# Retention outputs of layer 1 from centred values, with copies and squares moved to VectorE

## The chip, the cores and the metric

The kernel runs on one core of a Trainium2 chip. The metric is device time in microseconds of one execution. Engines: PE is TensorE (matmuls), DVE is VectorE, ACT is ScalarE, POOL is GpSimd, SP is SyncE, which here issues loads.

## The reference

One inference step of a 2-layer decoder, for a prompt of 256 tokens and 8 sample tokens that share all weights (264 columns in all, model width 1024). Each layer has three branches side by side (an S5 state space, stick-breaking attention and retention), then an output projection with a residual and a layer norm, then a feed-forward part with a short convolution. The change is in the retention branch of layer 1, whose core is this:

```python
def retention_branch(q, k, v, g, pos, s0, gn_g, gn_b):
    ...
    s_new, o = lax.scan(step, s0.astype(F32), (to_chunks(q), to_chunks(k), to_chunks(v)))
    o = o.swapaxes(0, 1).reshape(bn, L, RET_HEADS, RET_DV)
    mu = jnp.mean(o, -1, keepdims=True)
    var = jnp.mean(jnp.square(o - mu), -1, keepdims=True)
    o = ((o - mu) * lax.rsqrt(var + LN_EPS)).reshape(bn, L, RET_WIDTH) * gn_g + gn_b
    return jax.nn.silu(g) * o, s_new
```

Within a prompt, the output of a head is a weighted sum of value rows (`inner` times `v`), so its mean over the head's 128 features is the same weighted sum of the rows' means. The samples' outputs come from the state and the new value row. The other two branches end in an RMS norm.

## The kernel before

Features lie on the partitions, tokens in the columns: every activation is a tile of 128 x 264 (256 prompt columns, then 8 of samples). The weights are cut into units of 128 x 1024 that SP loads into a ring of five. A layer has 20 input units (`N_IN`), 8 output units (`N_OUT`), 44 up and 22 down. From unit 16 of layer 1 on, a weight is split in a rounded high half (ACT, `split_hi`) and the rest (DVE, `split_lo`), and each block is three matmuls: high by high, high by low, low by high.

Every engine has its own program, written out by hand, with semaphores between them (`need`, `E.did`). The table `AT` says behind which input tile `i` of a layer a step stands, and each engine goes through its steps in the order of its text; within an engine nothing overtakes. PSUM has eight banks, and `claim` waits for the last reader of a bank.

The tail of layer 1's input phase goes like this. Behind tile 16, TensorE turns the samples' outputs (`ret_samples_turn`, `sb_values_turn`), then transposes the value rows (`transposes`) and the samples' values (`v_samples`). ACT copies the values from PSUM to `VT` (`v_tokens`), copies the samples' rows and sends them to DRAM (`v_spread`); POOL fetches them back, spread over partitions, as `VBC` (`v_rows_back`). Behind tile 17, TensorE makes the retention outputs of the four heads from `VT` and the decayed scores `RI` (`ret_out`); ACT copies them into `Oh`, opens the first two gates (`open_gates`, with a table load on either side) and squares the second branch (`square_b`). Behind tile 18, TensorE multiplies `Oh` with a matrix of 1/128 for the means (`gn_means`), DVE subtracts them (`gn_center`), ACT squares, TensorE means again for the variance (`gn_vars`); between these stand the two branches' sums of squares (`rms`, which wait for `square_sum` on DVE). ACT takes logarithm and exponential into `rg`. Then come tile 19, the prompt's retention state (`ret_state`), and the output projection, whose first three tiles are done in two halves over the branches: `cat_hi` and `cat_lo` are their high and low halves, made by `branch_hi` on ACT and `branch_lo` on DVE behind `gn_scale` and `gn_out`.

DVE also updates the samples' retention states in `SR`, two operations for each of eight samples (`ret_states`); they wait for `VBC`. `STATES[L]` says which samples are done where: (4, 8) in layer 1 puts samples 0 to 3 ahead of the centring, 4 to 7 ahead of the branches' scaling, and none behind the splits. When all are done, POOL stores `SR` (1 MB). Behind the last low half DVE makes the low half of output unit 23 and adds the residuals; TensorE waits for the first of these (`z`) before it shifts the next norm and goes on to the fourth output.

Of the kernel before, what the change touches and what calls it, by code (L numbers as in the profile page):

```python
# [63 lines left out]
UP_BANKS = 8  # L64
SHIFTED = [4, 3]
END_BANK = [7, 0, 1, 2]
STATES = [(3, 5), (4, 8)]
SILU = [3, 2]
AHEAD = {j: 6 if j <= 24 else 4 for j in range(6, N_UP + 4)}
CSLOTS = 8  # L70
S5_ACT = [4, 6, 8]
# [35 lines left out]
def hybrid_step(nc, A, O):  # L107
    with ExitStack() as ctx:
# [12 lines left out]
        def at(name, shape, over=None, dt=F32):  # L121
# [4 lines left out]
            else:  # L126
# [33 lines left out]
        xe_hi = at("xe_hi", [P, KT, T], over=("z", 0), dt=F32R)  # L160
        ring_lo = at("ring_lo", [P, RING, 8, P], over=("ring", 0), dt=F32R)
        we_hi = [at(f"we_hi{e}", [P, 8, P], over=(home, plane * HJ * T), dt=F32R)
                 for e, (home, plane) in enumerate((("work", 0), ("work", 1), ("turn", 0), ("turn", 1)))]
        tabs = [(turn[:, 0, :, 0:SEQ], turn[:, 1, :, 0:SEQ]), None]
        RI = at("RI", [P, HEADS, DEC])
        KD = at("KD", [P, 2, 256])
        VT = at("VT", [P, 2, HEADS * DV])
# [46 lines left out]
        rope = at("rope", [P, 2, T])  # L214
        steps = at("steps", [P, SEQ])
        kdec = at("kdec", [P, 2, HEADS])
        vrow = at("vrow", [P, DV])
        gam = at("gam", [P, 1])
        gcol = at("gcol", [P, RAW, 2])
# [187 lines left out]
        def _(pe):  # L407
# [260 lines left out]

            def ret_out(L):
                need(pe, "vt", L, 2)  # L670
                for h in range(HEADS):
                    need(pe, "ri", L, h + 1)
                    bank = claim(OUT_BANK[h], "oev", L, h + 1)
                    mm(bank[:, 0:SEQ], VT[:, 0, h * DV:(h + 1) * DV], RI[:, h, 0:SEQ], start=True, stop=False)
                    E.did(mm(bank[:, P:SEQ], VT[:, 1, h * DV:(h + 1) * DV], RI[:, h, SEQ:DEC], start=False, stop=True),
                          "ro")

            def gn_means(L):
                need(pe, "osamp", L, 1)
                for h in range(HEADS):  # L680
                    need(pe, "oev", L, h + 1)
                    bank = claim(4 + h, "gd", L, h + 1)
                    E.did(mm(bank[:, 0:T], C["mean_v"], Oh[:, h], start=True, stop=True), "gmean")

            def gn_vars(L):
                for h in range(HEADS):
                    need(pe, "gsq", L, h + 1)
                    bank = claim(4 + h, "gv1", L, 1)
                    E.did(mm(bank[:, 0:T], C["mean_v"], sqo[:, h], start=True, stop=True), "gvar")

# [100 lines left out]
            for L in range(DEPTH):  # L791
# [7 lines left out]
                for i in range(RAW, N_IN):  # L799
                    out = claim(in_bank(i), "in_evac", L, i - RAW + 1)[:, 0:T]  # L800
                    if i in EARLY[L]:
                        tile8_split(L, i, out)
                    else:
                        tile8(L, i, out, lambda k: x[:, k],
                              (lambda k: need(pe, "x", L, k + 1)) if i == RAW else None)
                    for hf in range(2):
                        for c in range(2):
                            if i == at_[f"b{hf}{c}"]:
                                s5_b(L, hf, c)
                    if i == at_["ss"]:  # L810
# [24 lines left out]
                    if i == at_["sv"]:  # L835
                        sb_sample_values(L)
                    if i == at_["values"]:
                        sb_values(L)
                    if i == at_["rsq"]:
                        ret_samples(L)  # L840
                    if L == 0 and i == at_["out"]:
                        ret_out(L)
                    if i == at_["rt"]:
                        ret_samples_turn(L)
                    if i == at_["yt"]:
                        sb_values_turn(L)
                    if L > 0 and i == at_["vt"]:
                        transposes(L)
                    if L > 0 and i == at_["vb"]:
                        v_samples(L)  # L850
                    if L > 0 and i == at_["out"]:
                        ret_out(L)
                    if i == at_["gmean"]:
                        gn_means(L)
                    if i == at_["rms"]:
                        rms(L, sqa, 1, "rmsl", "rms", 2)
                        rms(L, sq2, 2, "rmsl", "rms", 3)
                    if i == at_["gvar"]:
                        gn_vars(L)
# [81 lines left out]
        def _(act):  # L941
# [14 lines left out]
            def split_hi_early(L, i):  # L956

                n = L * UNITS + i
                act.wait_ge(S(f"ld_w{ring_slot(n)}"), 16 * (n // RING + 1))
                need(act, "s5rd", L, 2)  # L960
                E.did(nc.scalar.copy(we_hi[EARLY[L].index(i)][:], ring[:, ring_slot(n)]), "w_hi")

            def upper_early(L):
# [182 lines left out]
            def v_tokens(L):  # L1146

                for tt in range(2):
                    need(act, "trv", L, tt + 1)
                    E.did(nc.scalar.copy(VT[:, tt], ps[:, 4 + tt]), "vt")  # L1150

            def v_spread(L):
                need(act, "vb", L, 1)
# [45 lines left out]
            for L in range(DEPTH):  # L1199
                at_ = AT[L]  # L1200
                ln_in(L)
                for i in range(RAW, N_IN):
# [82 lines left out]
                    if i == at_["out"]:  # L1285
# [3 lines left out]
                        if L == 0:  # L1289
                            square_a(L)  # L1290
                            split_hi(L, N_IN + 2)
                    if L > 0 and i == 17:
                        open_gates(L)
                        square_b(L)
                    if i == at_["gmean"]:
                        if L == 0:
                            square_b(L)
                        for h in range(HEADS):
                            need(act, "gd", L, h + 1)
                            E.did(f(sqo[:, h], Oh[:, h], ACT.Square), "gsq")  # L1300
                        if L > 0:
                            split_hi(L, N_IN + 2)
# [5 lines left out]
                    if i == at_["gvar"]:  # L1308
                        need(act, "gvar", L, HEADS)
                        E.did(f(rg[:], ps[:, 4:8, 0:T], ACT.Ln, bias=eps_t[LN_EPS]), "gv1")  # L1310
                        E.settle()
                        E.did(f(rg[:], rg[:], ACT.Exp, scale=-0.5), "gr")
                        for k in range(4):
                            branch_hi(L, k)
                E.settle()
                gates = hb[:, GC + SILU[L]:GC + HEADS]
                E.did(f(gates, gates, ACT.Silu), "gsil")
# [65 lines left out]
        def _(dve):  # L1383
# [504 lines left out]
            def sb_cat(L):  # L1888
                need(dve, "rmsr", L, 1)
                for t in range(2):  # L1890
                    E.did(stt(hb[:, QB_ + t], yb[:, t], pv(L, "norm_b_g", t), rms2[:, 1], ALU.mult, ALU.mult), "catb")

            def gn_center(L, heads):
# [17 lines left out]
            def branch_lo(L, k):  # L1911

                need(dve, "cat_hi", L, k + 1)
                E.did(tt(cat_lo[:, k], cat[k], cat_hi[:, k].bitcast(F32), ALU.subtract), "cat_lo")  # L1914

            def s5_skip(L, hf):
# [32 lines left out]
            for L in range(DEPTH):  # L1949
# [45 lines left out]
                    ret_states(L, range(0, STATES[L][0]))  # L1995
                else:
                    split_lo(L, N_IN)
                sample_out(L)
                sb_sample_out(L)
                if L > 0:  # L2000
                    split_lo(L, N_IN + 1)
                square_sum(L, 0)
                if L > 0:
                    ret_states(L, range(0, STATES[L][0]))
                gn_center(L, (0, 1))
                square_sum(L, 1)
                gn_center(L, (2, 3))
                if L == 0:
                    split_lo(L, N_IN + 1)
                ret_states(L, range(STATES[L][0], STATES[L][1]))  # L2010
# [244 lines left out]
```

## Time and profile before

| | us |
|---|---|
| median of 3 runs | 677.65 (677.31 to 677.99) |
| the profiled execution | 677.52 |
| its span, first to last instruction | 675.7 |

| engine | busy us | share of the span |
|---|---|---|
| TensorE, matmuls | 664.1 | 98% |
| VectorE | 566.6 | 84% |
| ScalarE | 415.7 | 62% |
| GpSimd | 90.7 | 13% |

The span is what the profiler saw of that execution; the rest of its time lies before the first and behind the last instruction. Times below are microseconds from the span's start. TensorE's granted clock is full in the whole span. Busy shares are averages; where an engine stands is seen only in the views of waits and of the chain, and when it does what in the timeline. In a timeline, instructions of one kind that follow each other are merged, "x8" is their count, and the time beside it is from the first start to the last end, or the sum where they overlap; a float32 matmul shows as two records.

### The profile page before, as it was taken

Reading aid. Unit: us, or ns where it says so; the run is one execution under the profiler, and the core shown is the slowest. Engines: PE = TensorE matmul, PEld = TensorE weight load, DVE = VectorE, ACT = ScalarE, POOL = GpSimd, SP = SyncE. Lnnn points to the kernel's source line nnn. Section 1 sums busy time; section 2 is a strip of 40 time slices with the busy share of each in tenths; the row PEclk is TensorE's granted clock in tenths of the full one; section 3 lists DMA queues with packets and bytes.
Section 4 is the critical chain, followed back from the end, with each engine's and each line's share of the span. In section 5 each row is a group of like instructions: output and inputs, shape, how many; then the busy total and the mean of one; then the engine's idle time right before and its main releaser. Section 6 shows DMA issues by size and latency. Waiting matters only on the chain. (4 is left out here: it accounts for less than half of the span.)

```text
span 675.7 us, 13394 instructions
## 1 busy us (share of the span) xinstructions
PE 664.1 (98%) x5030; PEld 615.2 (91%) x5030; DVE 566.6 (84%) x1191; ACT 415.7 (62%) x682; POOL 90.7 (13%) x90
## 2 busy tenths in 40 slices
PE   9999999999999999999999999899999999999997
PEld 7777887989999999999977887889999999999996
DVE  6999999989998988789489998688999898884653
ACT  5776258767765766645756445687767666663343
POOL 0000010140222211200200000105012222220001
PEclk9999999999999999999999999999999999999999
DMA  8776630746574555554365662454765545555411
GB/s 326 247 258 219 200 117 5 287 109 234 200 258 150 206 188 184 180 186 152 125 207 198 191 207 100 129 215 137 192 207 205 188 161 200 177 193 191 159 59 65
DMA packets 42916, 121.82 MB, mean 180 GB/s; under 512 B 5539, under 2 KB 15171, under 8 KB 42339
## 3 DMA queue, kind: packets, MB, share of 16 engines
q1 hardware_dynamic: 40466, 115.22, 49.5%
q0 software_dynamic: 1088, 4.11, 2.6%
q10 hardware_dynamic: 1296, 1.63, 0.8%
q8 instruction: 40, 0.66, 0.4%
q14 instruction: 26, 0.21, 0.1%
HBM read 115.33 MB, written 5.61 MB: 179 GB/s over the span
## 5 line engine op out<-in xcount | busy, mean ns | idle before, releaser
L1556 DVE TENSOR_TENSOR w_lo<-ring,w_hi 128x1024 fp32r<-128x1024 f32 x144 | 175.6, 1221 | 31.6 <-ACT w_hi L954 29.8
L436 PE MATMUL ps<-x_hi,w_hi 128*128 128x264 f32 x672 | 191.0, 284 | 1.0 <-DVE x_lo L1506 1.0
L437 PE MATMUL ps<-x_lo,w_hi 128*128 128x264 f32 x672 | 190.4, 283 | 0.0
L438 PE MATMUL ps<-x_hi,w_lo 128*128 128x264 f32 x672 | 190.3, 283 | 0.0
L954 ACT CAST w_hi<-ring 128x1024 fp32r<-128x1024 f32 x144 | 150.2, 1043 | 60.7 <-PE ps L438 59.6
L436 PEld LDWEIGHTS ps<-x_hi,w_hi 128*128 128x128 f32 x672 | 126.6, 188 | 1.8 <-issue 1.8
L437 PEld LDWEIGHTS ps<-x_lo,w_hi 128*128 128x128 f32 x672 | 126.6, 188 | 0.0
L438 PEld LDWEIGHTS ps<-x_hi,w_lo 128*128 128x128 f32 x672 | 126.0, 187 | 0.0
L429 PE MATMUL ps<-x,ring 128*128 128x264 f32 x480 | 112.1, 390 | 0.1
L429 PEld LDWEIGHTS ps<-x,ring 128*128 128x128 f32 x480 | 89.1, 190 | 18.9 <-issue 2.2
L436 PE MATMUL ps<-hff_hi,w_hi 128*128 128x264 f32 x352 | 100.0, 284 | 0.0
L438 PE MATMUL ps<-hff_hi,w_lo 128*128 128x264 f32 x352 | 99.9, 284 | 0.0
L437 PE MATMUL ps<-hff_lo,w_hi 128*128 128x264 f32 x352 | 99.9, 284 | 0.0
L2133 POOL TENSOR_TENSOR hff_lo<-conv,hff_hi 128x264 fp32r<-128x264 f32 x44 | 52.7, 1197 | 214.7 <-ACT hff_hi L1191 214.7
L438 PEld LDWEIGHTS ps<-hff_hi,w_lo 128*128 128x128 f32 x352 | 66.3, 188 | 0.0
L437 PEld LDWEIGHTS ps<-hff_lo,w_hi 128*128 128x128 f32 x352 | 66.2, 188 | 0.0
L436 PEld LDWEIGHTS ps<-hff_hi,w_hi 128*128 128x128 f32 x352 | 66.1, 188 | 0.0
L1342 ACT ACTIVATE conv<-ps,vec 128x264 f32<-128x264 f32 x84 | 47.8, 569 | 22.5 <-PE ps L438 22.5
L1191 ACT CAST hff_hi<-conv 128x264 fp32r<-128x264 f32 x44 | 18.2, 414 | 47.5 <-DVE conv L1577 47.3
L2060 DVE SCALAR_TENSOR_TENSOR conv<-ps,vec,conv 128x254 f32<-128x254 f32 x84 | 40.4, 481 | 3.0
L1206 ACT COPY hb<-ps 128x264 f32<-128x264 f32 x34 | 12.7, 373 | 45.5 <-PE ps L429 43.6
L2057 DVE SCALAR_TENSOR_TENSOR conv<-ps,vec,conv 128x255 f32<-128x255 f32 x84 | 39.8, 474 | 0.0
(349 smaller groups left out, 1090.1 us busy)
## 6 DMA issues: line engine op xcount, KB each, us to landing
ring<-in_units SPq DMA_DIRECT2D x187, 512.0 KB, 3.6
kv<-in_kpool SPq DMA_DIRECT2D x32, 128.0 KB, 2.2
kv<-in_vpool SPq DMA_DIRECT2D x32, 128.0 KB, 2.2
SR<-in_sret SPq DMA_DIRECT2D x2, 1024.0 KB, 6.0
out_rsample<-SR POOLq DMA_DIRECT2D x2, 1024.0 KB, 4.9
out_kv<-hb ACTq DMA_DIRECT2D x2, 528.0 KB, 4.4
VBC<-v_rows POOLq DMA_DIRECT2D x8, 128.0 KB, 3.1
out_y<-x SPq DMA_DIRECT2D x3, 264.0 KB, 2.1
```

What stands on the lines that cost most here:

```text
L429: ins = mm(out, ring[:, ring_slot(n), k], rhs(k), start=(k == 0), stop=(k == 7))
L436: mm(out, wh, hi, start=start, stop=False)
L437: mm(out, wh, lo, start=False, stop=False)
L438: return mm(out, wl, hi, start=False, stop=stop)
L954: E.did(nc.scalar.copy(w_hi[:, split_slot(i)], ring[:, ring_slot(n)]), "w_hi")
L1191: E.did(nc.scalar.copy(hff_hi[:, p], conv[:, (2 * p + 1) % CSLOTS]), "hff_hi")
L1206: E.did(nc.scalar.copy(hb[:, i], ps[:, in_bank(i), 0:T]), "in_evac")
L1342: E.did(f(conv[:, i % CSLOTS], source, ACT.Identity, scale=pv(L, "cw2", i), bias=pv(L, "cb", i)), "fc")
L1556: E.did(tt(w_lo[:, slot], ring[:, ring_slot(L * UNITS + i)], w_hi[:, slot].bitcast(F32), ALU.subtract), "w_lo")
L2057: E.did(stt(c[:, 1:SEQ], bank[:, 0:SEQ - 1], pv(L, "cw1", i), c[:, 1:SEQ], ALU.mult, ALU.add))
L2060: E.did(stt(c[:, 2:SEQ], bank[:, 0:SEQ - 2], pv(L, "cw0", i), c[:, 2:SEQ], ALU.mult, ALU.add), "up_free")
L2133: E.did(tt(hff_lo[:, p], conv[:, (2 * p + 1) % CSLOTS], hff_hi[:, p].bitcast(F32), ALU.subtract), "hff_lo")
```

## The change

In layer 1 alone (`CENTRED`):

- TensorE transposes the value rows ahead of the two turns. ACT copies them in eight pieces of 128 columns (token half by head), each with its sum over the row (`vsum`). DVE subtracts the mean of each row and head (`center_values`) into a second tile `VTc`, and `ret_out` reads that, behind a new wait. `ret_state` still reads `VT`.
- The prompt's columns of `Oh` are then centred as they come. `gn_means` becomes one matmul over the 32 sample columns, DVE centres these (`gn_center_samples`), ACT squares the prompt's columns in two pieces behind the gates and the samples' in a third.
- DVE takes over the copies of `Oh` (`ret_outputs`) and the squares and sum of the second branch (`square_b`). ACT opens the gates directly behind its copy of tile 17.
- State updates: samples 0 to 3 between the centring and the branches' scaling, 4 to 7 behind the low half of output unit 23, ahead of the first residual.
- ACT's split of output unit 22 moves from ahead of the branch norms to behind the high halves of branches 0 to 3.
- `VTc` takes the place of the fourth early weight's high half, which moves to `work`; the low half of branch 4 waits for tile 19 therefore, and the early high halves wait for the rotary step.

```diff
-STATES = [(3, 5), (4, 8)]
+STATES = [(3, 5), (0, 4)]
+CENTRED = [False, True]
...
-                 for e, (home, plane) in enumerate((("work", 0), ("work", 1), ("turn", 0), ("turn", 1)))]
+                 for e, (home, plane) in enumerate((("work", 0), ("work", 1), ("turn", 0), ("work", 3)))]
+        VTc = at("VTc", [P, 2, HEADS * DV], over=("turn", HJ * T))
...
             def ret_out(L):
                 need(pe, "vt", L, 2)
+                values = VTc if CENTRED[L] else VT
+                if CENTRED[L]:
+                    need(pe, "gd", L, 2)
...
             def gn_means(L):
                 need(pe, "osamp", L, 1)
+                if CENTRED[L]:
+                    bank = claim(4, "gd", L, 3)
+                    E.did(mm(bank[:, 0:HEADS * NS], C["mean_v"], Oh[:, :, SEQ:T], start=True, stop=True), "gmean")
+                    return
...
-                    need(pe, "gsq", L, h + 1)
+                    pe.wait_ge(S("gsq"), HEADS * L + (1 if CENTRED[L] else h + 1))
...
+                    if L > 0 and i == at_["vt"]:
+                        transposes(L)
                     if i == at_["rt"]:
                         ret_samples_turn(L)
                     if i == at_["yt"]:
                         sb_values_turn(L)
-                    if L > 0 and i == at_["vt"]:
-                        transposes(L)
...
-                    E.did(nc.scalar.copy(VT[:, tt], ps[:, 4 + tt]), "vt")
+                    if CENTRED[L]:
+                        for h in range(HEADS):
+                            part = slice(h * DV, (h + 1) * DV)
+                            ins = f(VT[:, tt, part], ps[:, 4 + tt, part], ACT.Copy, accum_out=vsum[:, tt, h:h + 1])
+                    else:
+                        ins = nc.scalar.copy(VT[:, tt], ps[:, 4 + tt])
+                    E.did(ins, "vt")
...
                     if L > 0 and i == 17:
                         open_gates(L)
-                        square_b(L)
+                        if CENTRED[L]:
+                            for h in (0, 2):
+                                need(act, "oev", L, h + 2)
+                                E.did(f(sqo[:, h:h + 2, 0:SEQ], Oh[:, h:h + 2, 0:SEQ], ACT.Square))
...
+                        if CENTRED[L]:
+                            need(act, "gd", L, 3)
+                            E.did(f(sqo[:, :, SEQ:T], Oh[:, :, SEQ:T], ACT.Square), "gsq")
...
-                        if L > 0:
-                            split_hi(L, N_IN + 2)
...
                         for k in range(4):
                             branch_hi(L, k)
+                        if L > 0:
+                            split_hi(L, N_IN + 2)
...
+            def ret_outputs(L):
+                for h in range(HEADS):
+                    need(dve, "ro", L, h + 1)
+                    E.did(cp(Oh[:, h, 0:SEQ], ps[:, OUT_BANK[h], 0:SEQ]), "oev")
+            def square_b(L):
+                need(dve, "ybs", L, 1)
+                E.did(tt(sq2[:], yb[:], yb[:], ALU.mult))
+                E.settle()
+                E.did(tt(sq2[:, 0], sq2[:, 0], sq2[:, 1], ALU.add), "sqsum")
+            def center_values(L):
+                for k in range(2):
+                    need(dve, "vt", L, k + 1)
+                    E.did(stt(VTc[:, k].rearrange("p (h e) -> p h e", h=HEADS), bcast(vsum[:, k], [P, HEADS, DV], 2),
+                              -1.0 / DV, VT[:, k].rearrange("p (h e) -> p h e", h=HEADS), ALU.mult, ALU.add), "gd")
+            def gn_center_samples(L):
+                dve.wait_ge(S("gmean"), HEADS * L + 1)
+                o = Oh[:, :, SEQ:T]
+                E.did(tt(o, o, ps[:, 4, 0:HEADS * NS].rearrange("p (h b) -> p h b", h=HEADS), ALU.subtract), "gd")
...
                     split_lo(L, N_IN)
+                    center_values(L)
                 sample_out(L)
                 sb_sample_out(L)
                 if L > 0:
                     split_lo(L, N_IN + 1)
                 square_sum(L, 0)
                 if L > 0:
-                    ret_states(L, range(0, STATES[L][0]))
-                gn_center(L, (0, 1))
-                square_sum(L, 1)
-                gn_center(L, (2, 3))
+                    ret_outputs(L)
+                    square_b(L)
+                if CENTRED[L]:
+                    gn_center_samples(L)
...
                 ret_states(L, range(STATES[L][0], STATES[L][1]))
```

## Rows read from the trace of the kernel before

**Rows 1.** Waits of TensorE: line, releaser, us in total, times, longest.

```profile
PE ps L585 <- DVE sq L1901: 1.9, 1, 1.9
```

**Rows 2.** Chain of waits, 418 to 480: start, us, what.

```profile
426.42 1.54 DMA v_rows<-vrow
...
430.32 4.78 DMA VBC<-v_rows
435.24 2.19 DVE SR L1826 x8
...
441.92 1.04 ACT turn L1310
```

**Rows 3.** Timeline of TensorE, tail of layer 1: start, us, line, count, idle before.

```profile
423.86 0.38 PE L666 MATMUL ps<-cst,ots 128*128 128x128 f32 x2
...
424.51 1.04 PE L592 MATMUL ps<-cst,hb 128*128 128x128 f32 x8
...
428.86 0.59 PE L674 MATMUL ps<-RI,VT 128*128 128x256 f32 x2
...
434.37 1.94 PE L683 MATMUL ps<-Oh,cst 128*128 128x264 f32 x8
...
439.17 1.94 PE L689 MATMUL ps<-RI,cst 128*128 128x264 f32 x8
440.76 0.48 PE L448 MATMUL ps<-xe_hi,we_hi 128*128 128x264 f32 x1
...
445.09 0.36 PE L436 MATMUL ps<-cat_hi,w_hi 128*128 128x264 f32 x1
...
455.28 0.61 PE L460 MATMUL ps<-z,cst 128*128 128x264 f32 x2
...
470.24 1.96 PE L500 MATMUL ps<-zg,ring 128*128 128x266 f32 x8
...
472.92 0.61 PE L535 MATMUL ps<-acc,cst 128*128 128x264 f32 x2
```

**Rows 4.** Timeline of ScalarE, same stretch.

```profile
425.15 1.07 ACT L1150 COPY VT<-ps 128x512 f32<-128x512 f32 x2 [0.71 <-PE ps L592]
426.11 0.29 ACT L1156 COPY vrow<-ps 128x128 f32<-128x128 f32 x1
...
427.42 1.05 ACT L954 CAST w_hi<-ring 128x1024 fp32r<-128x1024 f32 x1 [1.03 <-DMA ring<-in_units]
...
432.06 1.28 ACT L1163 ACT_TABLE_LOAD   x1
...
434.02 1.28 ACT L971 ACT_TABLE_LOAD   x1
...
457.90 0.21 ACT L1000 COPY zg<-vec 128x16 f32<-128x16 f32 x1
```

**Rows 5.** Timeline of VectorE, same stretch.

```profile
409.04 0.68 DVE L1872 TENSOR_TENSOR ZT<-ZT,cst 128x512 f32<-128x512 f32 x1
...
425.74 1.22 DVE L1556 TENSOR_TENSOR w_lo<-ring,w_hi 128x1024 fp32r<-128x1024 f32 x1
...
441.95 0.90 DVE L1927 SCALAR_TENSOR_TENSOR hb<-yg,vec,rms 128x264 f32<-128x264 f32 x2 [0.61 <-ACT rms L1307]
...
444.11 0.49 DVE L1905 SCALAR_TENSOR_TENSOR Oh<-Oh,vec,turn 128x264 f32<-128x264 f32 x1 [0.45 <-ACT turn L1312]
...
453.49 0.42 DVE L1932 SCALAR_TENSOR_TENSOR z<-x,ps 128x264 f32<-128x264 f32 x1
...
460.05 0.43 DVE L1419 TENSOR_TENSOR z<-z,ps 128x264 f32<-128x264 f32 x1
...
470.44 0.43 DVE L1419 TENSOR_TENSOR z<-z,ps 128x264 f32<-128x264 f32 x1 [0.53 <-PE ps L438]
...
471.83 0.43 DVE L1435 TENSOR_TENSOR acc<-acc,sqt 128x264 f32<-128x264 f32 x1 [0.50 <-ACT sqt L979]
```

More of the change, by code:

```diff
@@ L216, in hybrid_step @@
         kdec = at("kdec", [P, 2, HEADS])
+        vsum = at("vsum", [P, 2, HEADS])
         vrow = at("vrow", [P, DV])
@@ L673, in ret_out @@
                     bank = claim(OUT_BANK[h], "oev", L, h + 1)
-                    mm(bank[:, 0:SEQ], VT[:, 0, h * DV:(h + 1) * DV], RI[:, h, 0:SEQ], start=True, stop=False)
-                    E.did(mm(bank[:, P:SEQ], VT[:, 1, h * DV:(h + 1) * DV], RI[:, h, SEQ:DEC], start=False, stop=True),
+                    mm(bank[:, 0:SEQ], values[:, 0, h * DV:(h + 1) * DV], RI[:, h, 0:SEQ], start=True, stop=False)
+                    E.did(mm(bank[:, P:SEQ], values[:, 1, h * DV:(h + 1) * DV], RI[:, h, SEQ:DEC], start=False, stop=True),
                           "ro")
@@ L960, in split_hi_early @@
                 need(act, "s5rd", L, 2)
+                need(act, "qk", L, 1)
                 E.did(nc.scalar.copy(we_hi[EARLY[L].index(i)][:], ring[:, ring_slot(n)]), "w_hi")
@@ L1284, in _ @@
                         split_hi(L, N_IN + 1)
-                    if i == at_["out"]:
+                    if L == 0 and i == at_["out"]:
                         for h in range(HEADS):
@@ L1288, in _ @@
                             E.did(nc.scalar.copy(Oh[:, h, 0:SEQ], ps[:, OUT_BANK[h], 0:SEQ]), "oev")
[L1289 to L1291 removed]
+                        square_a(L)
+                        split_hi(L, N_IN + 2)
                     if L > 0 and i == 17:
                         open_gates(L)
[L1294 removed]
+                        if CENTRED[L]:
+                            for h in (0, 2):
+                                need(act, "oev", L, h + 2)
+                                E.did(f(sqo[:, h:h + 2, 0:SEQ], Oh[:, h:h + 2, 0:SEQ], ACT.Square))
                     if i == at_["gmean"]:
@@ L1297, in _ @@
                             square_b(L)
-                        for h in range(HEADS):
-                            need(act, "gd", L, h + 1)
-                            E.did(f(sqo[:, h], Oh[:, h], ACT.Square), "gsq")
-                        if L > 0:
-                            split_hi(L, N_IN + 2)
+                        if CENTRED[L]:
+                            need(act, "gd", L, 3)
+                            E.did(f(sqo[:, :, SEQ:T], Oh[:, :, SEQ:T], ACT.Square), "gsq")
+                        else:
+                            for h in range(HEADS):
+                                need(act, "gd", L, h + 1)
+                                E.did(f(sqo[:, h], Oh[:, h], ACT.Square), "gsq")
                     if i == at_["rms"]:
@@ L1314, in _ @@
                             branch_hi(L, k)
+                        if L > 0:
+                            split_hi(L, N_IN + 2)
                 E.settle()
@@ L1891, in sb_cat @@
                     E.did(stt(hb[:, QB_ + t], yb[:, t], pv(L, "norm_b_g", t), rms2[:, 1], ALU.mult, ALU.mult), "catb")
+            def ret_outputs(L):
+                for h in range(HEADS):
+                    need(dve, "ro", L, h + 1)
[14 more added lines that the diff above has]
+                E.did(tt(o, o, ps[:, 4, 0:HEADS * NS].rearrange("p (h b) -> p h b", h=HEADS), ALU.subtract), "gd")
             def gn_center(L, heads):
@@ L1913, in branch_lo @@
                 need(dve, "cat_hi", L, k + 1)
+                if k == 4 and EARLY[L]:
+                    tile_done(dve, L, EARLY[L][-1])
                 E.did(tt(cat_lo[:, k], cat[k], cat_hi[:, k].bitcast(F32), ALU.subtract), "cat_lo")
@@ L2003, in _ @@
                 if L > 0:
-                    ret_states(L, range(0, STATES[L][0]))
-                gn_center(L, (0, 1))
-                square_sum(L, 1)
-                gn_center(L, (2, 3))
+                    ret_outputs(L)
+                    square_b(L)
+                if CENTRED[L]:
+                    gn_center_samples(L)
+                else:
+                    gn_center(L, (0, 1))
+                if L == 0:
+                    square_sum(L, 1)
+                if not CENTRED[L]:
+                    gn_center(L, (2, 3))
                 if L == 0:
```

## The prediction

> **What bounds the kernel now.** The busy table comes first: TensorE is busy 98% of the span, so time can only come from the few places where it waits or from work taken off it. The view of waits, TensorE's own, names such places; the longest is in layer 1: 1.9 us until VectorE has summed the second branch's squares [rows 1]. The chain of waits says why that sum is late. The value rows of layer 1 go out to DRAM, come back as VBC, and VectorE stands until 435.24 for them, since its order puts eight state updates (samples 0 to 3, 2.19 us) ahead of the norm's centring [rows 2]. From there the chain runs through the centring, the squares and the logarithm and exponential on ScalarE (441.92 to 444.11 [rows 2, 5]) to the scaling on VectorE, the high and low copies of the branches and the first output matmuls. TensorE has its output tiles to start on at 445.09, ends the first three at about 455.28 with short gaps, and from 455.28 to 470.24 has none [rows 3]. Behind the next norm the same view has no wait of TensorE in the up- and down-projections, so what layer 1's tail gains up to there is the gain of the kernel. Layer 0 keeps its code.
>
> **The change, part by part.**
>
> Means. Four matmuls with the mean matrix, from 434.37, become one over 32 columns. By starts, four such matmuls take some 1.8 us (the four variance matmuls, 439.17 to tile 19 at 440.76, take 1.6 to 1.8 [rows 3]); the small one I put at 0.25. TensorE is spared 1.5 us on top of the wait of 1.9 us.
>
> Transposes first. They started at 424.51, behind two groups of turns from 423.86 [rows 3]; they start 0.65 us sooner, and so the copies of values can begin at 424.50 instead of 425.15 [rows 4]. The turns come later by about a microsecond; sample_out, their reader, has its new place behind the centring, so that costs nothing.
>
> Value copies with sums. Two copies of 512 columns (1.07 us together) become eight of 128 with a sum over the row. No row has a copy with a sum. Nearest below: the plain copy of 128 columns from PSUM, 0.29 us, of which some 0.1 overlaps the next (the two copies sum to 1.07 but the next begins 0.96 behind) [rows 4]: 0.2 each if the sum is free, 1.6 in all. Nearest above: the copy and a second small instruction that writes the sum out, for which the smallest ScalarE row stands (128x16, 0.21 [rows 4]), with nothing overlapped: 0.5 each, 4.0 in all. I take 0.29 + 0.21 - 0.09 = 0.41, 3.3 us in all, since a sum can only be read when its copy is through. The values are then whole at 427.8 instead of 426.1. Behind them on ScalarE stand the copy of vrow and its DMA, and the split of unit 21, which waited for its load until 427.42 anyway.
> The Trainium skill ("VectorE: DVE Perf Modes", Two Vector instructions with no wait between them) says of VectorE that an operation that writes out its accumulator is two instructions; nothing of before shows it for ScalarE. The Trainium skill ("ScalarE: Activation LUTs", What ACT_TABLE_LOAD costs) gives 186 ns + 0.833 ns per column less 93 ns of overlap, by which a 128-column copy with a free sum is 0.2 us and the whole 1.6 us.
>
> Centred values. Two VectorE operations of 512 columns, 0.68 each by the nearest row [rows 5], behind the split that ends at 426.9 (425.74 + 1.13 to the next). The second waits for the whole of the values: 427.8 + 0.7 = 428.5. TensorE needs them for the retention outputs at 428.86 [rows 3], a new wait with 0.35 us in hand. Nothing on TensorE's path, up to 0.45 us per copy.
>
> Copies of outputs and second squares, on VectorE. Four copies, one add over 264 and one square over 528 columns: 4 x 0.35 + 0.7 + 0.4 = 2.5 us, from 430.8 (behind the split of unit 21 and the first square sum) to 433.4. The old stand of 5.2 us covers them, and tile 18 ends on TensorE only at 434.37. ScalarE is rid of the same copies, so its gates open at 429.5 and not at 432.06: load, gates, load take 432.06 to 435.3 there [rows 4], now 429.5 to 432.7, and the squares of heads 0 to 3 end at 433.9, ahead of the means.
> A rule speaks against this part. Between 432.06 and 434.02 lie one table load of 1.28 and 0.65 us of work, with no gap [rows 4]. The Trainium skill ("ScalarE: Activation LUTs", What ACT_TABLE_LOAD costs) puts a further 1380 ns of drain behind each load; two of them would end the squares at 436.7 and the variances would start 1.2 us later. The row disagrees, and the row decides.
>
> The norm. The small mean ends at 434.6; both branch sums' matmuls follow (0.45 each) to 435.5. Beside them VectorE subtracts 32 columns and ScalarE squares 32 (about 0.2 each), done at 435.4. Variances start at 435.5, before at 439.17: -3.7. Logarithm and exponential follow the last variance: gr at 439.7 instead of 444.1. Tile 19 and the prompt's state (440.76 to 445.09, 4.3 us [rows 3]) end at 441.6: TensorE is ready 3.5 us sooner.
>
> States 0 to 3. They wait for VBC as before, now behind the centring, and ahead of the scaling of branches. VBC's way starts at the copy of vrow, 427.8 instead of 426.11, so the first update stands at 436.9 instead of 435.24 and the last ends at 439.1. The four scalings of the branches (0.9 for two [rows 5]) end at 440.7. That, and not gr at 439.7, now releases the norm's scaling: 440.7 for 444.11 [rows 5], **-3.4 us**. From there to the last low half the order on VectorE is the old one, and ScalarE's side holds it: the split of unit 22 is ready at 442.1, before VectorE comes to it at 443.0, and the second gates at 444.4 before 445.0. TensorE, ready at 441.6 with 72 matmuls for the first three outputs (8.75 us at the pitch of 455.28 to 470.24, 120 in 14.5), could end them at 450.4; it follows the low halves as before: the first three outputs end at 455.28 - 3.4 = 451.9.
>
> States 4 to 7. Eight updates (2.19 us) move from VectorE's slack behind the norm to between the split of unit 23 and the first residual. That residual started at 453.49, ended at 453.9, and TensorE needs it at 455.28 to shift the next norm [rows 3, 5]: 1.4 us in hand, less than 2.19. **+0.75 us** of a new wait. Behind it VectorE is 2.2 us later against TensorE than it was: the fourth sum (460.05) comes at 458.9. From 460.05 to 470.44 [rows 5] VectorE needs 10.4 us with 0.5 us idle, so the last sum comes at 468.8, 1.1 us behind its tile, before 0.2. The sums' second matmul, at 472.92, had its input at 472.26 (471.83 + 0.43), 0.7 us sooner [rows 3, 5]; that is used up: **+0.25 us**. The 1 MB store of the states leaves at 452.5 instead of 441.6 and lands long before ScalarE needs it past 470; GpSimd's adds of squares behind it on its queue start at 457, so nothing waits there.
>
> **Sum.** -3.4 + 0.75 + 0.25 = -2.4 us. The profiled execution is 677.52 us (its span 675.7), 0.13 below the median of 677.65. By the median: 675.25.
>
> **Rivals.**
> (a) The sum on the copies is free: values whole at 426.1, VBC as before, states end at 437.4, branches at 439.1, and gr (439.7) is last. Scaling -4.35, TensorE's end of the first three -4.2, the same +1.0 behind: -3.2, 674.45. For it: the split-free row of 0.29; against: a sum has to be written somewhere.
> (b) The sum costs 0.5 to 0.7 per copy. Each 0.1 above 0.41 delays VBC by 0.8 us, and from 0.45 the retention outputs too: at 0.5, -1.6 (676.0); at 0.6, -0.8 (676.85).
> (c) Slower: the same mechanism from 0.7 per copy on. The values' copies then take over 5.6 us, VBC lands 4 us late, and the path states, branches, scaling comes back to 443.1; with the +1.0 of the moved states, 0.7 is the point at which nothing is left, and at 0.9 it is +1.5, 679.15. No ScalarE row of so small a shape is near that.
> (d) The later store of 1 MB meets the weight loads of the up-projection, and a high half on ScalarE comes late. Its load is issued at about 455 and had some 2 us in hand: 1 MB takes 3.5 to 5 us, so up to 2 us could come back: 675.3 to 677.3.
> (e) The moved states delay nothing (VectorE faster than I think), or twice as much: within 0.8 us of the forecast.
>
> **How the numbers follow.** Forecast 50% (with e), its own range 674.8 to 675.9; (a) 22%; (b) 15%; (c) 5%; (d) 8%. Range: to (a) with e, 674.0, and up to (b) at 0.6, 676.9. A measurement here tells about 0.2%, 1.36 us, from no change: faster is below 676.3. That has the forecast, (a), a fifth of (b) and half of (d), 0.79, less 0.03 for mechanisms not listed: 0.76; slower is (c), 0.05; within 0.2% the rest, 0.19.
>
> **What would show each step.** After the change: no TensorE wait at the branch sums; the means as one matmul of 32 columns at 434.4; values whole at about 427.8, with eight copies of 0.3 and perhaps eight small instructions between; the first state update at 436.9, still waiting for VBC; scaling of the norm at 440.7, released by VectorE itself and not by ScalarE; a new TensorE wait of 0.7 us for the first residual, at 452; a short one for the last sum near 469. Wrong would be: a wait at the retention outputs at 428.9, scaling released by ScalarE (then a), a ScalarE wait for a weight load near 462 (then d), or any change in layer 0.

## The result, and the profile after

The changed kernel takes 674.36 us (median of 4 runs, 673.75 to 674.94); the kernel before, on the same chip, 677.63. The ratio is 0.9943, with a 95% interval of 0.9931 to 0.9955: 3.9 us faster by the ratio, 3.3 by the medians, where -2.4 was forecast. The median lies in the stated range (674.0 to 676.9), next to its low end and next to rival (a); by the ratio the time would be 673.8, just below the range. The profiled execution took 674.94 us, with a span of 673.1.

Two of TensorE's waits in the changed kernel, the longest and the new one, from the view of waits (line, releaser, us in total, times, longest):

```profile
PE ps L503 <- DMA ring<-in_units: 1.6, 1, 1.6
...
PE ps L463 <- DVE z L1982: 0.6, 1, 0.6
```

The wait for the square sum [rows 1] is gone, and the new one for the first residual is there. The wait of 1.6 us is for the very first weight, at 7.69 in the span. The same first load made TensorE wait between nothing and 2.1 us from one profiled execution to the next, whatever the kernel; it has nothing to do with the change. So I compare stretches by the distance from the end of layer 1's tile 16: 423.86 before [rows 3], 424.76 after. This is **the anchor** below, and "11.25 behind the anchor" means 11.25 us later than it.

TensorE's timeline after, as in [rows 3] (start, us, line, what, count, idle before):

```profile
424.76 1.04 PE L595 MATMUL ps<-cst,hb 128*128 128x128 f32 x8
...
429.76 0.60 PE L680 MATMUL ps<-RI,VTc 128*128 128x256 f32 x2
...
435.29 0.30 PE L688 MATMUL ps<-Oh,cst 128*128 128x32 f32 x2
...
436.40 1.94 PE L699 MATMUL ps<-RI,cst 128*128 128x264 f32 x8
437.98 0.48 PE L451 MATMUL ps<-xe_hi,we_hi 128*128 128x264 f32 x1
...
442.27 0.39 PE L439 MATMUL ps<-cat_hi,w_hi 128*128 128x264 f32 x1
...
451.75 0.28 PE L441 MATMUL ps<-cat_hi,w_lo 128*128 128x264 f32 x1
452.65 0.71 PE L463 MATMUL ps<-z,cst 128*128 128x264 f32 x2 [0.62 <-DVE z L1982]
...
467.70 1.96 PE L503 MATMUL ps<-zg,ring 128*128 128x266 f32 x8
...
470.39 0.61 PE L538 MATMUL ps<-acc,cst 128*128 128x264 f32 x2
```

The row at 467.70 begins the first tile of the up-projection, which is made from the residuals before their norm is known; I call it the **raw tile**. The norm's two sums are matmuls that stand between its blocks, and the last row is the second of them. It stands 45.63 us behind the anchor; before it stood 49.06 behind it (472.92 - 423.86 [rows 3]). **The change gains 3.43 us there**, and the rest of the span is as long as it was: 202.8 us behind that row before, 202.7 after. That agrees with the 3.3 us of the medians.

ScalarE, as in [rows 4]; a sum is an instruction of its own:

```profile
425.40 0.28 ACT L1164 ACTIVATE VT<-ps 128x128 f32<-128x128 f32 x1
425.57 0.19 ACT L1164 ACTIVATION_READ_ACCUMULATOR VT<-ps 128x1 f32 x1
425.67 0.27 ACT L1164 ACTIVATE VT<-ps 128x128 f32<-128x128 f32 x1
...
427.41 0.31 ACT L1173 COPY vrow<-ps 128x128 f32<-128x128 f32 x1
...
430.36 1.28 ACT L1180 ACT_TABLE_LOAD   x1
431.65 0.64 ACT L1180 ACTIVATE hb<-hb 128x528 f32<-128x528 f32 x1
432.31 1.28 ACT L982 ACT_TABLE_LOAD   x1
```

And VectorE, as in [rows 5]:

```profile
427.79 1.29 DVE L1933 SCALAR_TENSOR_TENSOR VTc<-vsum,VT 128x512 f32<-128x512 f32 x2
...
436.01 2.19 DVE L1849 SCALAR_TENSOR_TENSOR SR<-VBC,hb,SR 128x128 f32<-128x128 f32 x8 [0.20 <-DMA VBC<-v_rows]
...
440.68 0.49 DVE L1953 SCALAR_TENSOR_TENSOR Oh<-Oh,vec,turn 128x264 f32<-128x264 f32 x1 [0.86 <-ACT turn L1333]
...
450.07 2.19 DVE L1849 SCALAR_TENSOR_TENSOR SR<-VBC,hb,SR 128x128 f32<-128x128 f32 x8
452.17 0.42 DVE L1982 SCALAR_TENSOR_TENSOR z<-x,ps 128x264 f32<-128x264 f32 x1
```

Two readings matter for the forecast. The first state update stands 11.25 us behind the anchor; before it stood 11.38 behind it, though the rows were copied 0.4 us later (2.65 behind the anchor, before 2.25). And the norm's scaling is released by ScalarE's exponential with VectorE idle for 0.86 us: not by the state updates and branches, as the forecast had it.

### The profile page after: what moved, and what is told of

The parts are those of the page before. It is cut to its first block and busy times, and to the rows that moved or that the text cites. A ratio compares the mean times of both kernels' runs of the same rounds, so it can differ in the third digit from the quotient of the medians.

```text
span 673.1 us, 13390 instructions
## 1 busy us (share of the span) xinstructions
PE 661.4 (98%) x5024; PEld 613.4 (91%) x5024; DVE 569.1 (85%) x1195; ACT 415.2 (62%) x690; POOL 91.2 (14%) x90
## 5 line engine op out<-in xcount | busy, mean ns | idle before, releaser
L503 PE MATMUL ps<-zg,ring 128*128 128x266 f32 x160 | 39.0, 388 | 1.6 <-DMA ring<-in_units 1.6
```

The source lines that it names most:

```text
L503: ins = mm(out[:, 0:GB], ring[:, ring_slot(raw_unit(q, i)), k], zgs[q % 2][:, k], start=(k == 0), stop=(k == KT - 1))
```

## The experiments

All times are medians beside runs of the kernel before on the same chip (677.8 to 678.0 in these sets), and the ratios are to that kernel. In the code cuts "..." stands for lines left out. "Behind the anchor" is measured in each kernel's profiled execution, and D is the distance to the second sum: 49.06 before, 45.63 after.

**The changed kernel again.**

> The changed kernel once more, beside the others of this set. Both theories: 674.4 us, within 0.6 of it; the scaling of the norm released by ScalarE's exponential, and a TensorE wait of 0.6 us for the first residual.

674.6 us, ratio 0.9953 (0.994 to 0.9967), D 45.62. The scaling waits 0.69 us for the exponential, and TensorE 0.64 for the residual. The stretch repeats to 0.01 us; the whole time does not, because of its start.

**Are the sums on the path?** The copies without sums:

```diff
-                            ins = f(VT[:, tt, part], ps[:, 4 + tt, part], ACT.Copy, accum_out=vsum[:, tt, h:h + 1])
+                            ins = f(VT[:, tt, part], ps[:, 4 + tt, part], ACT.Copy)
...
+            E.did(nc.vector.memset(vsum[:], 0.0))
```

> The eight copies of layer 1's value rows without their sums (the row means are taken as zero, so the outputs of layer 1 are not centred). Theory of the prediction (the way of the value rows through DRAM, the state updates and the branches' scaling set the start of the norm's scaling): the copies end 0.8 us sooner, so 0.8 us faster than the changed kernel. Rival (the exponential on ScalarE is last, and the way through DRAM has 0.9 us in hand): the same time within 0.2 us, and VectorE stands 0.8 us longer ahead of the norm's scaling, or the landing does not move.

674.55 us, ratio 0.9951 (0.9937 to 0.9965), D 45.63. ScalarE's timeline:

```profile
426.84 1.47 ACT L1164 ACTIVATE VT<-ps 128x128 f32<-128x128 f32 x8
428.32 0.27 ACT L1173 COPY vrow<-ps 128x128 f32<-128x128 f32 x1
```

Eight copies without sums take 1.48 us to the next instruction, eight with sums 2.01 (425.40 to 427.41 above). A sum costs 0.07 us, a copy with one 0.25. Taking them away gains nothing: the rival holds. (The profiled execution itself took 676.29 us, 1.7 above the median. Its loss lies at the first load, far ahead of the anchor, and is taken up in the last section.)

**Is the way of the rows on the path?** GpSimd is made late with the fetch:

```diff
+        pdum = at("pdum", [P, 2 * P])
...
                 pool.wait_ge(S("st_vrow"), 16 * (L + 1))
+                if L > 0:
+                    E.did(tt(pdum[:], dtab[:, 2], dtab[:, 3], ALU.add), "vbt")
+                    E.did(tt(zsb[:], dtab[:, 0], dtab[:, 1], ALU.add), "vbt")
```

> Two GpSimd additions of 256 columns ahead of the fetch of the value rows in layer 1 delay VBC by some 1.5 us (a GpSimd addition of 264 columns takes 0.75 in the trace); nothing else waits for them. Theory of the prediction: 1.5 us slower than the changed kernel, all of the delay. Rival: only what exceeds the 0.9 us in hand, some 0.6 us slower, and the norm's scaling released by VectorE's own branches instead of ScalarE's exponential.

674.4 us, ratio 0.995 (0.9936 to 0.9963), D 45.62. The delay did not arrive. GpSimd and VectorE, from the timelines:

```profile
431.79 1.97 POOL L2177 DMA_DIRECT2D VBC<-v_rows  x4
...
436.30 2.19 DVE L1850 SCALAR_TENSOR_TENSOR SR<-VBC,hb,SR 128x128 f32<-128x128 f32 x8 [0.83 <-DMA VBC<-v_rows]
```

The fetch begins 7.37 us behind the anchor (424.42 here), in the repeated kernel 5.43: 1.9 us later. The update starts 11.88 behind it, there 11.41: 0.5 us later. So both theories missed, since both took the landing to follow the issue. The time from issue to landing of the four transfers shrank, in the view of the tile VBC, from this in the changed kernel

```profile
DMA to landing us min/median/max: 4.0/4.0/4.2
```

to this:

```profile
DMA to landing us min/median/max: 2.7/2.8/2.9
```

Before the change, where the fetch began 4.99 us behind the anchor, the median was 4.7 us: the earlier the fetch, the longer it took. The windows of a microsecond of the changed kernel point at a reason (us, busy of each engine, granted clock, share of the DMA engines busy, GB/s):

```profile
431.76:432.76 1.00, 1.00 (x10) 0.95 (x9) 1.00 (x4) 0.98 (x2) 0.40 (x1) 1.00 1.01 414
432.76:433.76 1.00, 1.00 (x11) 1.00 (x10) 0.96 (x4) 0.99 (x2) 0.00 (x0) 1.00 1.12 357
433.76:434.76 1.00, 1.00 (x10) 1.00 (x10) 0.43 (x1) 1.00 (x2) 0.00 (x0) 1.00 0.77 180
```

The transfer engines are full (a share of about 1 is all 16 of them). The load of output unit 22 (512 KB) is issued when tile 17 is done, at 429.96, and the fetch of the rows begins at 430.19. In the delayed run the same load was issued 2.2 us ahead of the fetch.

**Is it that load?** SP holds it until VBC has landed:

```diff
                 for i in range(13, UNITS):
+                    if L > 0 and i == N_IN + 2:
+                        sp.wait_ge(S("ld_vb"), 16 * HEADS * (L + 1))
                     unit(L, i)
```

> The changed kernel with the load of layer 1's output unit 22 held until VBC has landed. Theory that this load shares the transfer engines with VBC, and so sets its landing: VBC's transfers take 2.8 us or less instead of 4.0, the first state update follows the centring with no wait for VBC. Rival (the landing is fixed by the way from the copy of the rows): 4.0 us as before. Both: the kernel's time stays at 674.4 within 0.4, since the exponential on ScalarE releases the scaling, and unit 22 is needed only seven us later.

674.87 us, ratio 0.9952 (0.9938 to 0.9965), D 45.64. The four transfers take 2.7 to 2.9 us, and the first state update follows the centring without a wait:

```profile
435.76 2.19 DVE L1851 SCALAR_TENSOR_TENSOR SR<-VBC,hb,SR 128x128 f32<-128x128 f32 x8
...
440.70 0.49 DVE L1955 SCALAR_TENSOR_TENSOR Oh<-Oh,vec,turn 128x264 f32<-128x264 f32 x1 [0.96 <-ACT turn L1335]
```

The load is the cause of the slow landing in the changed kernel: that is shown, and it costs the kernel nothing now, since the exponential is last. For the kernel before it is argued, not run: there the same load was issued 0.2 us behind the fetch (429.05 and 428.85).

**What would my own price of the copies have done?** Four more copies between the two halves make the values 1.4 us late:

```diff
                     E.did(ins, "vt")
+                    if CENTRED[L] and tt == 0:
+                        for h in range(4):
+                            E.settle()
+                            E.did(f(zsb[:, 0:DV], VT[:, 0, 0:DV], ACT.Copy))
```

> The changed kernel with four more copies of 128 columns (0.3 us each, each waiting for the one before) between the two halves of layer 1's value copies: the price that the prediction gave to the sums, 1.3 us more than measured. Theory of the prediction: the values' way through DRAM, the state updates and the branches come 1.3 us later, 0.6 beyond the 0.7 in hand: the scaling 0.6 later, 675.1. Rival (the landing of VBC hangs on the load that shares the transfer engines): the first state update moves by less than 0.5 us, the scaling and the time not at all: 674.5. Both: the retention outputs still find the centred values in time, or wait up to 0.3 us.

674.44 us, ratio 0.9943 (0.9928 to 0.9959), D 45.87: 0.24 us more than the changed kernel in the stretch, below what the times can tell. The row copy is 1.4 us later than in the repeated kernel, the first state update 1.0 us (12.45 behind the anchor), the transfers took 3.2 us in the median. The scaling has no wait now: VectorE comes to it from the branches, at 16.17 behind the anchor, with the exponential done at 16.0 (the retention outputs were held up by 0.1 us for the centred values).

```profile
436.77 2.19 DVE L1853 SCALAR_TENSOR_TENSOR SR<-VBC,hb,SR 128x128 f32<-128x128 f32 x8 [1.31 <-DMA VBC<-v_rows]
...
440.49 0.49 DVE L1957 SCALAR_TENSOR_TENSOR Oh<-Oh,vec,turn 128x264 f32<-128x264 f32 x1
```

Here the forecast's mechanism is seen at work, and it is worth 0.24 us, not 0.9. Each expectation was right in part: the slack was used up, as the theory said, and the time hardly moved, as the rival said.

**The order of the state updates.** Samples 0 to 3 ahead of the centring again:

```diff
                 if CENTRED[L]:
+                    ret_states(L, range(0, 4))
                     gn_center_samples(L)
...
-                ret_states(L, range(STATES[L][0], STATES[L][1]))
+                if L == 0:
+                    ret_states(L, range(STATES[L][0], STATES[L][1]))
```

> The changed kernel with the state updates of samples 0 to 3 ahead of the centring again, as before the change. Theory that the order of the state updates carries the gain: centring ends 2.3 us later, the variances start 2.3 us later, 676.6 us. Rival that the gain is from the fewer and smaller mean steps and the earlier gates: within 0.5 us of the changed kernel.

677.7 us, ratio 0.9994 (0.998 to 1.0008), D 49.59: in the stretch the whole gain is gone, and 0.5 us more than it. TensorE waits 2.13 us for the squares, as forecast, and then it is slow:

```profile
438.07 3.61 PE L699 MATMUL ps<-RI,cst 128*128 128x264 f32 x8 [2.13 <-ACT RI L1319]
...
438.07:439.07 1.00, 1.00 (x2) 0.83 (x3) 0.00 (x0) 0.97 (x2) 0.00 (x0) 0.50 0.00 0
439.07:440.07 1.00, 1.00 (x4) 0.75 (x3) 0.76 (x2) 0.21 (x1) 0.00 (x0) 0.50 0.06 16
```

The granted clock is 0.50 (1.2 GHz) from the end of the wait, about 437.9, to about 441.3, where it was 1.00 (2.4 GHz) in the same stretch of the changed kernel. The eight records take 3.61 us instead of 1.94: 1.7 us on top of the 2.1. So of the 4.0 us by which D grew, 2.3 are the order and 1.7 the clock. The other executions agree: the two of the eleven with a mean clock of 0.999 or 1.000 took 676.5 and 676.8 us, as the order alone was expected to give (676.6); the nine from 0.995 to 0.998 took 677.3 to 679.0.

And the order alone, in the kernel before:

```diff
-STATES = [(3, 5), (4, 8)]
+STATES = [(3, 5), (0, 4)]
```

> The kernel before with one line of the change, the order of the state updates: samples 0 to 3 behind the centring, 4 to 7 behind the low half of output unit 23. Theory that this order carries the gain up to the next limit: TensorE's wait of 1.9 us for the second square sum goes, ScalarE's chain (gates, second squares, four squares, split of unit 22, logarithms) is next and brings the scaling some 1.9 us forward, the new wait for the first residual takes 0.7 back: 676.4. Rival (the order alone gives it all): 674.4. Rival (ScalarE's chain is already the limit): 677.6 or more.

677.12 us, ratio 0.9989 (0.998 to 0.9998), D 48.17: 0.9 us gained, 0.8 by the medians, where the theory expected 1.3. The scaling came 2.1 us sooner (18.11 behind the anchor), a little more than expected; 0.8 of it went to the new wait for the first residual and 0.45 to the steps up to the second sum. The order gives little by itself. The next limit is ScalarE, as expected (timeline):

```profile
434.88 1.28 ACT L971 ACT_TABLE_LOAD   x1
...
436.98 1.44 ACT L1300 ACTIVATE RI<-Oh 128x264 f32<-128x264 f32 x4
...
439.26 0.69 ACT L1305 ACTIVATE rms<-ps,eps_all 128x528 f32<-128x528 f32 x1
439.99 0.65 ACT L1307 ACTIVATE rms<-rms 128x528 f32<-128x528 f32 x1
440.54 1.13 ACT L1310 ACTIVATE turn<-ps,eps_all 128x1056 f32<-128x1056 f32 x1
```

There is no gap of ScalarE between the squares and the logarithm of the variances: the split of unit 22 stands in that row's place between them, and both branch logarithms behind it. TensorE waits here for the first residual too, and the norm's first sum starts 2.07 us behind the start of the raw tile (469.84 to 471.91) instead of 1.8.

**The other two parts.** The three mean matmuls kept, without use:

```diff
                 if CENTRED[L]:
+                    for h in range(1, HEADS):
+                        need(pe, "oev", L, h + 1)
+                        mm(claim(4 + h, "gv1", L - 1, 1)[:, 0:T], C["mean_v"], Oh[:, h], start=True, stop=True)
                     bank = claim(4, "gd", L, 3)
```

> The changed kernel with TensorE's other three mean matmuls of 264 columns kept (their results are not used). If the spared 1.3 us of TensorE lie on the path, the variances, the exponential and the scaling come 1.3 us later: 675.8. If not (another chain is as long), the time stays within 0.3 of the changed kernel.

675.78 us, ratio 0.9964 (0.9951 to 0.9977), D 46.96: 1.33 us, all three matmuls on the path.

And ScalarE with its old work (copies of the outputs ahead of the gates, the second branch's squares behind them):

```diff
                     if L > 0 and i == 17:
+                        for h in range(HEADS):
+                            need(act, "ro", L, h + 1)
+                            E.did(nc.scalar.copy(Oh[:, h, 0:SEQ], ps[:, OUT_BANK[h], 0:SEQ]), "oev")
                         open_gates(L)
+                        square_b(L)
...
-                    ret_outputs(L)
-                    square_b(L)
+                    square_sum(L, 1)
```

> The changed kernel with the copies of the outputs and the second branch's squares on ScalarE again, ahead of and behind the gates. Theory that ScalarE's relief carries the rest of the gain: gates open at 432.9 instead of 430.4, the sample squares end 2.2 us later, TensorE waits for them 1.5 to 2.2 us ahead of the variances: 676.6. If ScalarE had slack there: 674.5.

676.49 us, ratio 0.9979 (0.9969 to 0.9989), D 47.68: 2.05 us, as expected. TensorE waits 1.28 us for the second square sum and 0.25 for the sample squares, with its clock at 1.00 throughout.

**A better order.** Five samples ahead of the branches instead of four:

```diff
-STATES = [(3, 5), (0, 4)]
+STATES = [(3, 5), (0, 5)]
```

> The changed kernel with five samples' states ahead of the branches' scaling and three behind the low half of unit 23. If the 0.7 to 0.9 us in which VectorE stands for the exponential are free, the fifth sample (0.55 us) goes in there and TensorE's wait for the first residual falls from 0.6 to 0.1: 0.55 us faster than the changed kernel, 673.85. If that slack is not there, the scaling comes 0.5 later and nothing is gained.

674.02 us, ratio 0.9949 (0.9935 to 0.9962), D 45.12: 0.5 us better than the changed kernel. TensorE's wait for the residual is gone from the view of waits (by the starts, some 0.3 us of it is left: the shift stands 27.37 behind the anchor, in the next run 27.10), and the scaling still waits 0.17 us for the exponential. With the other three samples behind the first three residuals, one each:

```diff
-STATES = [(3, 5), (0, 4)]
+STATES = [(3, 5), (0, 5)]
...
-                ret_states(L, range(STATES[L][1], NS))
+                if L == 0:
+                    ret_states(L, range(STATES[L][1], NS))
...
+                    if L > 0 and i < 3:
+                        ret_states(L, range(5 + i, 6 + i))
                     if i in (5, 6):
```

> Five samples' states ahead of the branches' scaling, and the last three one by one behind the first three residuals. The wait for the first residual goes (0.6 us), the last sum is no later against its tile than now: 673.75. If VectorE's lag behind the output tiles mattered, part of this would come back at the norm's second sum.

673.89 us, ratio 0.9943 (0.9929 to 0.9956), D 45.10. The raw tile starts 42.06 behind the anchor instead of 42.94, but the norm's first sum comes 2.1 us behind that start instead of 1.8, so 0.3 of the 0.9 comes back there. It is no better than the simpler order. Both versions are faster than both kernels in the stretch; by their whole times the difference from the changed kernel, 0.3 to 0.7 us, is within the intervals.

## Why the prediction was right or wrong, point by point

**What bounds the kernel: right.** The wait, its cause in the order on VectorE, and TensorE as the limit elsewhere all stood. With the states back in their old place the same stretch lost 2.3 us by the order alone, and 1.7 more by TensorE's clock, which the forecast had no term for.

**Means: right.** The small matmul takes 0.14 us to the next start (435.29 to 435.43; I had put it at 0.25), and its three companions are worth 1.33 us in the experiment.

**Transposes first: right.** The value copies start 0.64 us behind the anchor, before 1.29.

**Copies with sums: the first term that was mis-sized.** I took copy and sum to be serial, 0.41 each, 3.3 us in all; they took 0.25 each, 2.0 in all. The sum is read by a second instruction, as the prediction assumed, but that one starts 0.17 us after its copy does, while the copy's own row is 0.28 long. The low bound of 0.2 each was nearer. The Trainium skill ("VectorE: DVE Perf Modes", Two Vector instructions with no wait between them) has the two instructions for VectorE; this trace shows them on ScalarE too. The estimate of 0.20 us for a copy without a sum, worked out in the prediction from the figures of the Trainium skill ("ScalarE: Activation LUTs", What ACT_TABLE_LOAD costs), compares with 0.18 measured.

**Centred values, outputs and squares on VectorE: right.** The centred values are whole 4.3 us behind the anchor and the retention outputs start 5.00 behind it, as before, with no wait. The copies of the outputs and the second squares end 9.4 behind it, forecast 9.5, and the gates' table load starts 5.60 behind it, forecast 5.64.

**States 0 to 3: the step that failed.** The forecast had the norm's scaling released by the branches, through "VBC's way starts at the copy of vrow, 427.8 instead of 426.11, so the first update stands at 436.9". ScalarE's exponential released it, and the scaling came 4.33 us sooner (15.92 behind the anchor, before 20.25), not 3.4. The first update stands 11.25 behind the anchor, forecast 13.04. Two terms made the difference.

The start of the way was mis-sized by the price of the copies: the rows are copied 2.65 behind the anchor, forecast 3.94. And the sentence moves the landing by the same amount as the start, which does not hold. From the copy of the rows to the first update it took 9.13 us before, 8.60 now and 8.4 with my dear copies. About half of that way is the four transfers, 4.7 us in the median before, with unit 22's load beside them, and 2.8 where the load was held. Holding the start back by 1.9 us moved the landing by 0.5.

The 0.93 us between forecast and measured scaling can't be split between the two terms by adding. With my price of the copies put back, the experiment has the scaling at 16.17, 0.25 later than in the changed kernel: the other 0.7 of the forecast's 16.84 is, but for a tenth, the way from the rows to the update. But an estimate from the same rows shows the other side, which no run tests: with the copies at the measured 0.25 each and the old way of 9.13, the first update stands at 11.8, the branches are done 3.8 us later at 15.6 (436.01 to 439.81 in the changed kernel), and the exponential, at 15.9, is last all the same. So the price of the copies alone, put right in the forecast's own sum, gives the right releaser and the whole of the missing 0.9.

**The norm, and ScalarE's part: right.** Variances start 11.64 us behind the anchor, forecast 11.64; the exponential is done at 15.9, forecast 15.8. The Trainium skill ("ScalarE: Activation LUTs", What ACT_TABLE_LOAD costs) and its drain behind each table load would, by the prediction's estimate, have put the variances 1.2 us later; load, gates and load follow each other at 430.36, 431.65 and 432.31 with no gap, so the row was rightly preferred.

**States 4 to 7: right in kind and size.** A new wait of 0.62 us, forecast 0.75; the first three outputs end 4.3 us sooner by the anchor and the shift of the norm starts 3.5 us sooner.

**The last sum: wrong by its whole 0.25 us.** I put the sum that makes the last residual 1.1 us behind its tile; it came at 468.28 for a tile that ended at 467.70, 0.6 behind, and the 0.7 us in hand covered that. The stretch from the first residual to the fourth sum took VectorE 6.2 us (452.17 to 458.39) and not 6.6: its stand of 0.46 us behind the third residual was no fixed cost. The mechanism exists: where the states were only moved in the kernel before, and where they were spread, the norm's first sum did come 0.3 us late.

**The sum and the chances.** The scaling came 4.33 us sooner; by the starts, the shift of the next norm lost 0.8 of that to the wait for the first residual, and 0.1 more was lost up to the raw tile: -4.33 + 0.8 + 0.1 = -3.43, against -3.4 + 0.75 + 0.25 = -2.4. That is close to rival (a)'s -3.2, and (a) had the right releaser. Its reason was not quite right: the sum was not free, but at 0.07 us it was too cheap to matter. (a)'s own sum also holds the +0.25 that did not come. (b) and (c), one in five together, rested on a price per copy that passes through to the end one for one. It doesn't: 1.4 us of delay in the copies cost 0.24. (d) did not happen: the store left at 452.55 and no wait for a load followed.

## What to carry to other kernels

A transfer's time in a trace belongs to the traffic beside it. Before moving its landing with its start, look at the busy share of the transfer engines in that window: where it is full, the landing may stay where it is, and a later start is free for a while. When a forecast takes the later of two chains that end close together, work out both with each doubtful price at its low and its high value, since a small price can change which of them is last. And a removed wait is worth no more than what is next: here the order of the updates alone gave 0.9 us, the other parts cost 1.3 and 2.0 when taken back one by one, and only together did they give 3.4. Such numbers don't add up, and what a part is worth depends on which others are in. Where a step is moved from one slack to another, measure both slacks and split it between them: one sample's update of 0.55 us put in the 0.7 us ahead of the scaling took away most of the new wait.

## What the runs showed of the hardware

- In two profiled executions TensorE stood for a little over 2 us, and its granted clock behind the wait was 0.50 (1.2 GHz): in the experiment with the early states behind 2.13 us, from about 437.9 to 441.3, where it cost 1.7 us more, and in the copies without sums behind 2.11 us for the first load, from about 7.8 to 11.2, where it cost 1.6 us more. This is the second, with its first full half microsecond:

```profile
7.92 1.25 PE L503 MATMUL ps<-zg,ring 128*128 128x266 f32 x2 [2.11 <-DMA ring<-in_units]
...
8.00:8.50 0.50, 0.50 (x1) 0.42 (x2) 0.00 (x0) 0.14 (x1) 0.00 (x0) 0.50 1.07 376
```

- The wait of 1.86 us in the kernel before had the clock at 1.00 behind it, and so had the changed kernel's 1.60 us at the same first load, and waits of 1.28 and 0.25 us in another run. So in these traces the two waits over 2 us cost nearly twice their length, and the shorter ones their length only.
- A ScalarE copy of 128 columns from PSUM costs 0.18 us in a row of eight, with a sum over the row 0.25; the reading of the sum is a row of its own, about 0.2 us long, most of it beside other work.
- Four 128 KB fetches took 2.8 us each in the median from issue to landing with the 512 KB load held back, and 2.8 too with it issued 2.2 us ahead of the first fetch. With the load issued 1.6 us ahead they took 3.2, with it 0.2 us ahead 4.0, and with it 0.2 us behind 4.7 (the kernel before) and 4.6 (its order alone changed).
